# Weighting expert rows at the PSUM exit and adding a token's second row by an adding gather

## The reference, cut to what matters

```
expert = grp[:, None] * EXPERTS_PER_GROUP + local
wts = jnp.take_along_axis(scores, expert, axis=1)
wts = wts / wts.sum(-1, keepdims=True)
...
def expert_block(args):
    xb, e = args
    hid = jax.nn.silu(xb @ w_gate[e]) * (xb @ w_up[e])
    return hid @ w_down[e]
...
out = jnp.zeros((N + 1, D), yb.dtype).at[tok_pad].add(yb * w_pad[:, None].astype(yb.dtype))
```

## Time and profile before

| | us |
|---|---|
| median of 3 runs | 2443.0 |
| lowest, highest | 2440.2, 2444.43 |
| the profiled execution | 2443.03 |
| its span, first to last instruction | 2441.4 |
| TensorE busy in the span | 2260.9 (93%) |
| DVE, ACT, POOL busy | 1330.0, 1098.4, 306.1 |
| granted TensorE clock, mean | 0.966 of 2.4 GHz |

### The profile page before, as it was taken

One profiled execution on the slowest core, in us unless ns is written; L12 is line 12 of the kernel. 1 busy time (PEld: TensorE's weight loads), 2 busy tenths in 40 slices (PEclk: granted clock), 3 DMA queues, 4 the chain that ended last, 5 costly groups with the idle time before them and its releaser, 6 DMA issues. The chain is left out here.

```text
span 2441.4 us, 39656 instructions
## 1 busy us (share of the span) xinstructions
PE 2260.9 (93%) x11838; PEld 1701.5 (70%) x11838; DVE 1330.0 (54%) x2251; ACT 1098.4 (45%) x1870; POOL 306.1 (13%) x387
## 2 busy tenths in 40 slices
PE   7999997889899999999798999999989899999974
PEld 4766665667688888887486565656678688888851
DVE  4222312576776756663683444433367677755757
ACT  3211212552346655663443443434343366754645
POOL 0000001670010000000100333000000011000003
PEclk8999999899999999999899999999999899999987
DMA  7566665665358767785456544333350378866846
GB/s 284 169 215 215 215 205 155 181 210 199 137 223 307 287 256 285 282 298 180 145 165 203 190 145 146 95 99 95 104 212 40 139 301 331 326 240 223 328 199 226
DMA packets 124693, 504.01 MB, mean 206 GB/s; under 512 B 19152, under 2 KB 39089, under 8 KB 105776
## 3 DMA queue, kind: packets, MB, share of 16 engines
q1 hardware_dynamic: 96270, 409.88, 47.7%
q0 software_dynamic: 18416, 64.11, 7.5%
q10 hardware_dynamic: 9906, 28.75, 3.2%
HBM read 437.13 MB, written 73.42 MB: 209 GB/s over the span
## 5 line engine op out<-in xcount | busy, mean ns | idle before, releaser
L2263 DVE TENSOR_TENSOR e_wl<-e_raw_gate_up,e_wh 128x1024 fp32r<-128x1024 f32 x256 | 298.5, 1221 | 88.4 <-ACT e_wh L2171 88.0
L2082 PE MATMUL e_psG<-e_wh,e_xh 128*128 128x512 f32 x784 | 315.8, 403 | 9.2 <-issue 7.6
L2084 PE MATMUL e_psG<-e_wh,e_xl 128*128 128x512 f32 x784 | 307.3, 392 | 0.0
L2083 PE MATMUL e_psG<-e_wl,e_xh 128*128 128x512 f32 x784 | 306.5, 391 | 0.0
L2171 ACT CAST e_wh<-e_raw_gate_up 128x1024 fp32r<-128x1024 f32 x256 | 251.2, 1046 | 63.9 <-DMA e_raw_gate_up<-in_e_gate 24.2
L2082 PEld LDWEIGHTS e_psG<-e_wh,e_xh 128*128 128x128 f32 x784 | 147.9, 189 | 39.0 <-issue 9.3
L2084 PEld LDWEIGHTS e_psG<-e_wh,e_xl 128*128 128x128 f32 x784 | 147.5, 188 | 32.2
L2083 PEld LDWEIGHTS e_psG<-e_wl,e_xh 128*128 128x128 f32 x784 | 148.1, 189 | 28.4
L2263 DVE TENSOR_TENSOR e_wl<-e_raw_down,e_wh 128x1024 fp32r<-128x1024 f32 x128 | 153.1, 1218 | 15.1 <-ACT e_wh L2171 15.1
L615 PE MATMUL in_ps<-in_w_upper,in_h_upper 128*128 128x512 f32 x384 | 155.3, 404 | 3.3 <-DVE in_h_lower L335 2.8
L2082 PE MATMUL e_psY<-e_wh,e_hh 128*128 128x512 f32 x392 | 154.0, 393 | 2.8 <-DVE e_hl L2286 2.8
(11 more groups left out here) (616 smaller groups left out, 4570.9 us busy)
## 6 DMA issues: line engine op xcount, KB each, us to landing
e_raw_gate_up<-in_e_gate SPq DMA_DIRECT2D x32, 2048.0 KB, 10.0
e_raw_gate_up<-in_e_up SPq DMA_DIRECT2D x32, 2048.0 KB
e_raw_down<-in_e_down SPq DMA_DIRECT2D x32, 2048.0 KB
x<-in_ada_w SPq DMA_DIRECT2D x40, 1024.0 KB, 5.3
yrows<-e_y ACTq DMA_DIRECT2D x49, 512.0 KB, 8.7
x<-in_cache SPq DMA_DIRECT2D x64, 320.0 KB
a_pages<-in_cache SPq DMA_DIRECT2D x64, 320.0 KB, 3.5
qkvo<-in_out SPq DMA_DIRECT2D x48, 256.0 KB, 2.3
```

The costliest lines, as they stand in the source:

```text
L2082: T.matmul(out, upper[:, k, :], wh[:, z, cols], start=k == 0, stop=False)
L2083: T.matmul(out, upper[:, k, :], wl[:, z, cols], start=False, stop=False)
L2084: mm = T.matmul(out, lower[:, k, :], wh[:, z, cols], start=False, stop=k == PIECES * n - 1)
L2263: V.tensor_tensor(wl[:, z, at], raw[z][:, at], wh[:, z, at].bitcast(F32), ALU.subtract).then_inc(s_lo[z], 1)
```

## The change

Rows are weighted when they leave PSUM. For that the routing builds a weight for each slot and row, in the way in which `tokens` is built: GpSimd multiplies `hot_slot` by the weights into a new `hot_weight`, TensorE multiplies that by `hot_row` in 18 plain fp32 matmuls (not fp32r), and DVE copies the sum to `row_weight`. `weigh` moves ahead of the wait for `tokens`. `hot_slot` now stays a one-hot array, and its product with the token numbers goes to `hot_id`. Both combining stages lose `first` on ACT and the weighting on DVE. The first two tiles' rows are still gathered apart and added by DVE; for the other seven tiles the second gather adds to what the first has written, so it waits until that has landed. The last combine has six buffers of `z` in place of four each of `z`, `ya` and `yb`; the latents' stage now uses all four halves of `y`.

```
             po.wait_ge(s_tok, 1)
             gather(tokens[:, 0:1])
+            po.wait_ge(s_norm, 1)
+            nc.gpsimd.tensor_tensor(hot_weight[:].rearrange("p k t s -> p (k t) s"),
+                                    hot_slot[:].rearrange("p k t s -> p (k t) s"),
+                                    g.weight[:].rearrange("p k t -> p (k t)").unsqueeze(2).broadcast_to([P, 2 * TILES, SLOTS]),
+                                    ALU.mult).then_inc(s_hw, 1)
...
             turn_x(0)
-            keep_warm(T, g, psG[:, 1, 0:P], 3)
+            pe.wait_ge(s_hw, 1)
+            pe.wait_ge(s_tok, 1)
+            for k in range(2):
+                for t in range(TILES):
+                    mm = T.matmul(psH[:, 1, 0:SLOTS], hot_row[:, k, t, :].bitcast(F32), hot_weight[:, k, t, :],
+                                  start=(k == 0 and t == 0), stop=(k == 1 and t == TILES - 1))
+            mm.then_inc(s_wsum, 1)
             gate(0, 0)
...
                 for z in range(2):
-                    S.copy(y[:, z * HALF:(z + 1) * HALF], psY[:, z, :])
+                    S.activation(y[:, z * HALF:(z + 1) * HALF], psY[:, z, :], ACT.Copy, scale=row_weight[:, bass.ds(b, 1)])
...
             count()
+            weigh()
             v.wait_ge(s_num, 1)
...
             lower(GATE, 0, range(3, PIECES))
-            weigh()
-            v.drain()
+            v.wait_ge(s_wsum, 1)
+            V.tensor_copy(row_weight[:], psH[:, 1, 0:SLOTS]).then_inc(s_rw, 1)
             lower(UP, 0)
```

The last combine, GpSimd and the start of a tile on DVE:

```
+            def first(t):
+                if t >= RING:
+                    po.wait_ge(s_cen, t - RING + 1)
+                    po.wait_ge(s_ss, t - RING + 1)
+                gather(t, 0, zr[:, t % RING, :], s_a[t])
+
+            def second(t):
+                po.wait_ge(s_a[t], 16)
+                gather(t, 1, zr[:, t % RING, :], s_b[t], ALU.add)
+
+            for t in range(APART):
+                first(t)
+                gather(t, 1, yb[:, t, :], s_b[t])
+            for t in range(APART, TILES, 2):
+                both = range(t, min(t + 2, TILES))
+                for j in both:
+                    first(j)
+                for j in both:
+                    second(j)
...
-                v.drain()
+                v.wait_ge(s_a[t], 16)
+                v.wait_ge(s_b[t], 16)
+                if t < APART:
+                    V.tensor_tensor(z, z, yb[0:n, t, :], ALU.add)
+                    v.drain()
                 V.tensor_tensor(z, z, gate[0:n, t // PT, :], ALU.mult)
```

The stage with the latents, GpSimd:

```
             for i in range(2, TILES):
-                po.wait_ge(s_mid, i - 1)
-                gather(i)
+                if i < 4:
+                    po.wait_ge(s_gated, i - 1)
+                else:
+                    po.wait_ge(s_mid, i - 3)
+                gather(i, 0, rows_y(i), s_a[i])
+                po.wait_ge(s_a[i], 16)
+                gather(i, 1, rows_y(i), s_b[i], ALU.add)
```

More of the change, by code:

```diff
@@ L2376, in weigh @@
                     V.tensor_tensor(g.weight[:, k, :], g.weight[:, k, :], ws[:], ALU.mult)
+                v.drain()
+                V.memset(g.weight[NSAMP:P, :, TILES - 1:TILES], 0.0).then_inc(s_norm, 1)
             def count():
@@ L2570, in _ @@
             S.copy(both_rows[:], lb33[:]).then_inc(s_row, 1)
-            for t in range(3):
-                first(t)
             for t in range(TILES):
@@ L2889, in upper @@
                 act.sem_inc(s_up, 1)
-            def first(i):
-                t, n = i, rows_of(i)
-                act.wait_ge(s_g[i % 2], 32 * (i // 2) + 32)
-                S.activation(y[0:n, i % 2, 0, :], y[0:n, i % 2, 0, :], ACT.Copy,
-                             scale=g.weight[0:n, 0, t:t + 1]).then_inc(s_first, 1)
             def deviation(i):
@@ L3011, in gated @@
                 t, n = i, rows_of(i)
-                z = y[0:n, i % 2, 0, :]
-                v.wait_ge(s_first, i + 1)
-                V.scalar_tensor_tensor(out=z, in0=y[0:n, i % 2, 1, :], scalar=g.weight[0:n, 1, t:t + 1], in1=z,
-                                       op0=ALU.mult, op1=ALU.add)
-                v.drain()
+                z = rows_y(i)
+                v.wait_ge(s_a[i], 16)
+                v.wait_ge(s_b[i], 16)
+                if i < 2:
+                    V.tensor_tensor(z, z, y[0:n, i, 1, :], ALU.add)
+                    v.drain()
                 if t == PT:
```

96 lines of the change are left out of this document (39 added, 57 removed).

## The result

| | before | changed |
|---|---|---|
| median, us | 2445.77 (15 runs) | 2456.14 (15 runs) |
| lowest, highest | 2440.2, 2451.37 | 2447.93, 2467.17 |
| profiled execution, its span | 2443.03, 2441.4 | 2453.48, 2451.6 |
| granted clock, mean | 0.966 | 0.962 |

The ratio is 1.0039, with a 95% interval of 1.0028 to 1.005: the changed kernel is 7 to 12 us slower. I had predicted 2436.3, with 2446.0 as the upper end. Beside the slower median stands a wider spread, 19 us instead of 11. It belongs to the answer.

What follows compares the result with a forecast made beforehand. TensorE was taken to bound the kernel nearly everywhere, except the last combine, where DVE's chain of waits does. The terms +4.9 + 0.2 - 4.6 - 7.2 = -6.7 against 2443.03 gave 2436.3 us, range 2430.5 to 2446.

Steps and rivals of the forecast that it cites:

- Part 1, own time: Routing, both layers: 18 new matmuls make 36 records taking 4.0 us, so `gate(0, 0)` starts 2.4 us later.
- Part 1, the step that failed: Routing into experts: TensorE has no gap until the stage ends, so the 2.4 us delay stays in each layer.
- The term +4.9: Routing of two layers together: +4.9 us, range 0.8 to 7.4.
- `weigh` and GpSimd's product: Routing: `weigh` fits DVE's 1.00 us wait; GpSimd's product takes 1.4 to 1.5 us, free with 2.5 us of cover.
- Part 2: Experts: weighting on ACT costs 0.1 us a slot, hidden by TensorE except at the last slot; +0.2 us.
- Part 3: Combine with latents: ACT no longer waits for rows, so TensorE starts earlier; -4.6 us, range -6 to 0.
- Part 4, DVE alone: Last combine: if DVE alone sets the pace, tile 8's gate comes at 2418.5 instead of 2429.03, gaining 10.6 us.
- Part 4, the gathers: Last combine: rounds of 8.0 to 10.0 us for two tiles, adding priced between free and double; gain 7.2 us.
- (B): Rival: adding costs double and tile 1 lands 1.6 us later; sum -1.9, 2441.1 us; chance 0.20.
- (C): Rival: last combine slower, queue works adding gathers row by row, 7 us each; sum +6.6, 2449.6 us; chance 0.12.
- (A): Rival: gathers keep up, last combine is DVE's alone, gain 10.6; sum -11.1, 2431.9 us; chance 0.18.
- (D): Rival: GpSimd's product in the routing starts 6 us late, TensorE waits 3.3 us a layer; 2442.9 us; chance 0.08.

Runs made afterwards that it cites:

- b_narrow: Kernel before, with 18 f32 products of 128x32, result unused, replacing the three pairs of fillers in each layer's routing; 2454.79 us, ratio 1.0048.
- c_bypass: Changed kernel, its seven adding gathers of the last combine replaced by plain ones, same rows, order and waits; 2446.42 us, ratio 1.0012.
- c_ring9: Changed kernel with nine z buffers in the last combine, all first rows asked for before the first adding gather; 2448.61 us, ratio 1.0018.
- b_dense: Kernel before, with ten pairs of 128x128 clock-keeping products instead of three behind the turn of x; 2447.33 us, ratio 1.0005.

## Why the prediction was wrong

- **Part 1, own time: right.** 36 records took 4.10 us (4.0 predicted), and the first `gate` product comes 4.86 us behind the start of the turn (695.06 - 690.20) instead of 2.49, 2.4 later.
- **Part 1, the step that failed.** "As TensorE has no gap until the stage ends, the 2.4 stay": the sum prices everything behind the new products at full speed, and TensorE's clock isn't a term of it. The new products let the clock fall: about 1.5 us a layer in every profile with the stretch there, and 1.3 more as the mean over the layers in which it falls earlier and those in which it doesn't. The term +4.9 measured about +10 (b_narrow, 9.7). The old trace could have warned: its 22 fillers behind 18 narrow products took 4.33 us, 0.197 a record, where the prediction itself worked out 0.10 from the later ones.
- **`weigh` and GpSimd's product: right on time,** 686.81 to 688.0, ready 3 us before TensorE comes to it. That it holds DVE for 1.2 us wasn't foreseen; there it was free.
- **Part 2: about right.** The weighted move off PSUM takes 1.26 us for a slot's two halves against 1.07, 0.2 a slot instead of 0.1, and the slots still follow each other every 17.72 us.
- **Part 3: mechanism right, size too large.** The first l_psK product comes 23.0 us after the first gather (1192.93 - 1169.89) instead of 25.7: 2.7 won, not 4.6. The step is "DVE can start `gated(1)` when tile 1 has landed", 17.6 us after the first gather. The addition starts at 1189.57, 19.7 after it, but only 0.8 of that is waiting for rows: DVE itself had been busy until 18.9 (1188.74) with its share of tile 0 and of the weights. So most of the 2.1 us lie in DVE's own program, which I had taken as ready, and the rest in the later landing ("may take back up to 1.7"). The stage as a whole gained 2.1 and 4.0 in these two profiles.
- **Part 4, DVE alone: about right.** 4.26 us a tile, and tile 8's gate at 43.0 after the first gather once what the four waits have beyond the usual 0.2 (11.5 us) is taken off 54.6; I had 2418.5 - 2376.17 = 42.3. Tile 0's addition starts 0.9 later than I had it, 7.6 instead of 6.7.
- **Part 4, the gathers: the second step that failed.** "I take the middle between free and double" and "a round of 8.0 to 10.0 us". An adding gather cost double (1.55 us of all 16 engines more, on 1.56), which I had at a gain of 4, and the rounds took 11 to 14: 2389.62, 2400.83, 2414.95 and 2426.51 are the issues of their first gathers. I had priced the bytes and the rounds apart, each as if the other were free. They act together: with the adding taken out the waits fall by 8.2 us of 12.8 (c_bypass), with the rounds taken out by 3.1 (c_ring9). The median landing was no longer than before, 7.0 us against 7.5; but a round holds two landings in series, and tile 4 took 10.4 us for the first (2400.83 to 2411.22) and 6.9 for the second (to 2418.09). This is the larger of the two misses. In place of -7.2 stand +1.8 and +1.0 in the two profiles of the changed kernel.
- **The rivals.** (B) had the right price for the adding in this order and for tile 1, but no term for the clock; with its 5.6 us (2 x 2.8) the sum of -1.9 would have been +3.7. (C) has the nearest number, 2449.6, and the last combine did end later than before, but its mechanism didn't happen: in c_ring9 the seven adding gathers were all down within 27.8 us of the first one's issue (2398.67, the last issued at 2409.84, the longest landing 16.6), 4.3 a tile against the 4.8 for an adding gather alone from which (C) decides. (A) and (D) didn't happen.

The sum with the terms as measured: 10.4 (routing) + 0.2 - 3 (latents, the mean of 2.1 and 4.0) + 1.4 (last combine, the mean) = 9.0, against a measured 10.4 between the medians. Against the forecast of 2436.3, then, the last combine is worth 8.6 us of the miss, the routing 5.5, the latents 1.6; 2.7 more are the before kernel's median of 15 runs, 2445.77 instead of 2443.03, and 1.4 stay unexplained. What stays open is why in some executions the clock falls within the stretch and in others only behind it. No run here tells this.

## What to carry to other kernels

A stretch of narrow products on TensorE has a second price, the clock behind it: whoever puts one where filler stood should look what the clock does behind such a stretch that the kernel already has, and price the products behind the new one at 1.2 GHz if it falls. A busy share of 100% doesn't show it, only the granted clock does. An adding gather moves work from a compute engine to the DMA engines at up to twice a gather's price and puts two landings in series. The one order here in which DVE never waited for it had it only where those engines are idle, with its first gather a tile ahead. And when a mended wait gives back less than its length, look at who is late next: here first DVE behind GpSimd, then TensorE behind ACT.

## What the runs showed of the hardware

- TensorE busy for 4.00 of 4 us with f32 products of 32 columns: the granted clock fell from 1.00 right behind them in 10 of 16 layers (0.57 over the next 4 us) and inside them in 6. With 18 one-record products in 2.47 us it fell too. In the kernel before it fell behind the 18 fp32r products, under 22 filler records without a gap (0.64, then 0.51). Twenty filler records in the place of the narrow ones, 2.40 us (b_dense), left it at 1.00. The Trainium skill, page TensorE: Matmul & The Clock Gate, Part 1, says that activity releases the throttle; what these rows add is that the busy time alone doesn't tell when the clock falls.
- The 64-column products cost what the 32-column ones do: 18 in 2.17 us against 2.15.
- An indirect gather that adds took the DMA engines about twice a plain one's time for the same packets and bytes in the changed kernel (1.55 us more on 1.56), and 1.06 more in c_ring9. The Trainium skill's DMA: Bandwidth & Descriptors, Rules for kernel authors, has the read and the later write of the destination; 36.7 against 26.6 us of all 16 engines agrees with it.
- One GpSimd product of 576 elements a partition held DVE's operation beside it for nearly its whole length of 1.16 to 1.17 us: 1.38 us instead of 0.18, 1.83 instead of 0.83.
